# Scatter of the expert outputs issued behind the eight picks of a pass instead of directly behind the gather

## What is computed

```python
logits = xt @ w_router + b_router
top_v, top_i = lax.top_k(logits, 4); gates = softmax(top_v)
def expert_block(idx, gate, e):
    xb = xt[idx]                                   # gather of token rows
    g = min(xb @ w_gate[e] + b_gate[e], 7); u = clip(xb @ w_up[e] + b_up[e], -7, 7)
    y = (g * sigmoid(1.702 * g) * (u + 1)) @ w_down[e] + b_down[e]
    return y * gate
out = x + segment_sum(all blocks' y by token)      # scatter with addition
```

## Time and profile before

| | |
|---|---|
| time, median of 3 runs | 2278.34 us (2276.03 to 2282.03) |
| the profiled execution's own time | 2279.51 us |
| its span in the profile | 2277.8 us |
| PE busy | 96% of the span |
| DVE, ACT, POOL busy | 68%, 50%, 38% |
| from the gather of iteration 1 to the scatter behind the loop | 894.82 to 2212.10 us |

### The profile page before, as it was taken

One profiled execution on the slowest core, in us unless ns is written; L12 is line 12 of the kernel. 1 busy time (PEld: TensorE's weight loads), 2 busy tenths in 40 slices (PEclk: granted clock), 3 DMA queues, 4 the chain that ended last, 5 costly groups with the idle time before them and its releaser, 6 DMA issues.

```text
span 2277.8 us, 36180 instructions
## 1 busy us (share of the span) xinstructions
PE 2196.1 (96%) x11524; PEld 1552.7 (68%) x11525; DVE 1547.1 (68%) x1940; ACT 1128.4 (50%) x1130; POOL 857.1 (38%) x484
## 2 busy tenths in 40 slices
PE   8999999999999969999999999999999999999997
PEld 6874554787888747777666667666676766667775
DVE  5534443444344588888777878787788777788885
ACT  4432333423231145776555656565565565665664
POOL 1333120000000034656444555354555554455651
PEclk9999999999999979999999999999999999999999
DMA  6421111232333368999887888888898888798896
GB/s 233 90 76 46 46 37 29 75 101 84 100 113 130 131 261 276 362 337 333 299 285 271 295 304 305 291 310 302 303 333 294 295 299 302 269 303 319 323 336 193
DMA packets 206013, 517.82 MB, mean 227 GB/s; under 512 B 19168, under 2 KB 86624, under 8 KB 205952
## 3 DMA queue, kind: packets, MB, share of 16 engines
q1 hardware_dynamic: 190016, 470.97, 57.0%
q0 software_dynamic: 15936, 46.02, 9.4%
HBM read 480.68 MB, written 32.05 MB: 225 GB/s over the span
## 4 chain that ended last, share of the span: by engine, by line
PE 82%; DVE 7%; DMA 5%; issue 3%; ACT 2%; SPq 0%; POOL 0%; DVEq 0%; ACTq 0%; POOLq 0%
PE psum L1800 14%; PE psum L1802 12%; PE psum L1801 12%; PE psum L1623 7%; PE psum L1811 5%; DMA ring<-in_w_up 5%; PE psum L1645 4%; DVE w_lo L1336 4%; PE psum L1643 4%; PE psum L1644 4%; PE psum L1850 3%; PE psum L1567 2%; PE psum L1566 2%; PE psum L1568 2%; PE psum L1729 1%
## 5 line engine op out<-in xcount | busy, mean ns | idle before, releaser
L1336 DVE TENSOR_TENSOR w_lo<-ring,w_hi 128x2048 fp32r<-128x2048 f32 x384 | 874.8, 2301 | 110.1 <-ACT w_hi L882 98.9
L882 ACT ACTIVATE w_hi<-ring 128x2048 fp32r<-128x2048 f32 x384 | 728.5, 1920 | 370.9 <-DMA ring<-in_w_up 250.4
L646 POOL TENSOR_SCALAR pick<-iota_bf,slot_col 128x256 bf16<-128x256 bf16 x244 | 468.9, 1936 | 141.8 <-DVE slot_col L1349 141.8
L1800 PE MATMUL psum<-w_hi,xT_hi 128*128 128x512 f32 x1008 | 417.9, 415 | 29.7 <-DVE w_lo L1336 24.6
L1802 PE MATMUL psum<-w_hi,xT_lo 128*128 128x512 f32 x1008 | 401.7, 399 | 0.0
L1801 PE MATMUL psum<-w_lo,xT_hi 128*128 128x512 f32 x1008 | 401.4, 398 | 0.0
L1800 PEld LDWEIGHTS psum<-w_hi,xT_hi 128*128 128x128 f32 x1008 | 191.0, 189 | 142.4 <-issue 59.2
L652 POOL DMA_INDIRECT xg<-h_rows,idx_new x32 | 71.8, 2243 | 490.9 <-DVE idx_new L1330 473.3
L1800 PE MATMUL psum<-w_hi,aT_hi 128*128 128x512 f32 x528 | 221.3, 419 | 8.5 <-issue 4.5
L1802 PEld LDWEIGHTS psum<-w_hi,xT_lo 128*128 128x128 f32 x1008 | 191.6, 190 | 46.6
L1801 PEld LDWEIGHTS psum<-w_lo,xT_hi 128*128 128x128 f32 x1008 | 191.8, 190 | 39.8
(11 more groups left out here) (333 smaller groups left out, 3240.2 us busy)
## 6 DMA issues: line engine op xcount, KB each, us to landing
ring<-in_w_gate SPq DMA_DIRECT2D x256, 512.0 KB, 5.1
ring<-in_w_up SPq DMA_DIRECT2D x256, 512.0 KB, 6.4
ring<-in_w_down SPq DMA_DIRECT2D x256, 512.0 KB, 5.4
ring<-in_w_in SPq DMA_DIRECT2D x44, 512.0 KB, 5.1
ring<-in_x SPq DMA_DIRECT2D x16, 512.0 KB, 3.6
ring<-in_w_in SPq DMA_DIRECT2D x6, 1024.0 KB, 6.5
vb<-oT SPq DMA_DIRECT2D x16, 256.0 KB, 6.4
ring<-in_w_oc SPq DMA_DIRECT2D x16, 256.0 KB, 2.9
```

Source lines behind the costliest of these rows:

```text
L646: e.tensor_scalar(pick[:, t, :], iota_bf[:, :], slot_col[:, t, :], None, ALU.is_equal).then_inc(g_pick, 1)
L882: e.activation(w_hi[:, hs, :], ring[:, slot, :], ACT.Copy).then_inc(g_hi, 1)
L1336: e.tensor_tensor(w_lo[:, hs, :], ring[:, slot, :], w_hi[:, hs, :].bitcast(F32), ALU.subtract).then_inc(g_lo, 1)
L1800: e.matmul(dst, hi, w_up, start=start, stop=False)
```

## The change

POOL issues the scatter after the eight picks instead of between the gather and the picks. The wait for its landing and the raising of `g_free` follow directly. Two conditional blocks become one.

```diff
             with e.Fori(0, n_loop) as p:
                 gather(p + 2, False)
+                pick_tokens(p + 3)
                 with e.If(p > 0):
                     scatter(p)
-                pick_tokens(p + 3)
-                with e.If(p > 0):
                     scattered(p)
                 e.sem_inc(g_free, 1)
```

## The result

The changed kernel takes 2375.18 us (2372.24 to 2383.90, 4 runs) against 2278.99 us before: ratio 1.0425, 95% interval 1.0405 to 1.0445. It is 96 us slower. The prediction had the sign and the mechanism, but 17 us for the size, and a range that ended at 2321.

A forecast was written before the change was run, and what follows sets the result against it. PE was taken to bound the kernel, with 82% of the chain. Lateness of 19.7 us, less 7.0 for the removed collision, plus 4.3 for the clock, gave 17 us slower: 2295 us, range 2273 to 2321.

The forecast's parts named there:

- Where the loss would come from: At the pass end, DVE's `shift_rows` waits for `g_free` behind picks and scatter landing, delaying the next pass: 19.7 us.
- That the picks would not begin earlier: On POOL, picks still wait for `slot_col` and begin 14 to 15 us after the gather, so nothing is gained there.
- The hand-overs: Three steps, from picks to scatter and from landing over `g_free` to DVE, estimated at 0.9 us together.
- The landing of the pair: Both scatters issued and landed behind the picks in 8.4 us, taken from the scatter behind the loop; bounds 7.0 to 12.5.
- the subtraction of the prediction: POOL's idle time before each gather set against a 12.0 us chain; shortfalls, with the last pass, total 19.7 us.
- The room behind the picks: POOL's idle time before the next gather: 6.95 to 11.81 us in short passes, 12.79 or more in the others.
- the collision: Scatter packets delay weight loads in the first third of a pass; removing this was to give back 7.0 us.
- The clock: PE gaps at pass boundaries lower its granted clock; half of five shortfalls at 1.7 us each, 4.3 us.
- A longer chain: Rival: scatter issue or landing stretched behind the picks, 10.4 us for the pair; +47 us, 2325 us; chance 0.12.
- Faster: Rival: the pair lands within 5 us, nothing is late, PE's waits inside passes go; 2265 us; chance 0.14.
- just fits: Rival: the pair needs 7.0 us and hand-overs 0.6, lateness 9.0 against up to 12.5 gained; 2275 us; chance 0.18.
- The signs in the profile: Short passes become 42 to 43 us, long ones keep their length; PE's mid-pass waits shrink, ACT's `in_w_up` waits fall.

## Why the prediction was right in kind and wrong in size

- **Where the loss would come from.** Right: picks, issue, landing, `g_free`, `shift_rows`, and with it `row_numbers`, the gather and the first `w_lo`. The copy of the row numbers took that wait out and 86 of the 96 us with it.
- **That the picks would not begin earlier.** Right: 14.6 us after the gather.
- **The hand-overs, 0.9 us.** Too large. The scatter is issued 0.17 us behind the picks, and `shift_rows` starts within about 0.2 us of the landing.
- **The landing of the pair, 8.4 us. This step failed first.** In the pass shown it is 945.35 - 933.45 = 11.9 us up to the copy on DVE. I had taken the one scatter behind the loop for the nearest row, and set aside the landings of up to 9.7 us in the loop as being due to the gather ahead of them. With no gather ahead the median is 9.4 us, above that of before (7.7 us). So the queue behind the gather was not what made them long. The addition has about 2 us of it; what the rest is stays open. A fuller stream of loads is not shown: the DMA engines were as busy during the one scatter behind the loop, though they moved fewer bytes then (length, engines, PEclk, DMA share, GB/s; the kernel after, then before):

```profile
933.40:945.30 11.90, 4.84 (x36) 3.31 (x34) 1.12 (x2) 5.29 (x4) 3.21 (x2) 0.91 1.04 322
```

```profile
2212.10:2220.50 8.40, 8.40 (x37) 6.76 (x36) 8.05 (x6) 4.72 (x3) 3.53 (x2) 1.00 1.01 271
```

The need is then 0.2 + 11.9 + 2.7 = 14.8 us instead of 12.0. This pass is a fair sample: in the 13 late passes that a gather follows, it came 12.8 to 16.4 us behind the last pick, 14.8 on average. With that, the subtraction of the prediction over the idle times of before gives 51 us in 14 passes instead of 19.7 in eight.
- **The room behind the picks. The second step that failed.** I took it from the kernel before and made it smaller only where I credited a gain. But without the collision the short passes are shorter still, and most of them have longer picks: in the pass shown for the run without a scatter there are 6.88 us of room, where there were 13.71. Of the 107.2 us of waiting, this is the other half. In the 14 late passes the eight picks took 18.5 us on average, against 16.1 in the same passes of the kernel before: 33 us, which I had put at nothing. The relief (20.4 us by the run without a scatter, where I had counted 7.0 in the sum) could not show as time, because a pass in which the chain is the longest path can't use it; I count it as waiting on DVE. 51 + 33 + 20 = 104 us. The run without a scatter gives the same from the other side: its room falls short of 14.8 us in the same 14 passes, by 120 us together, and 2257.4 + 120 is 2377 us, where 2373.3 were measured.
- **The clock, 4.3 us.** Under-sized. PE's busy time in the loop grew by 12.7 us against before. The gaps at the boundaries were 5 to 11 us long, not 3 to 4. The granted clock was low for longer than the 3.4 us of the earlier trace rows: 0.66 as a mean over 15 us is about 10 us at the lower level. But more than half of that lay in the gap, where it costs nothing. The clock was low before PE began again at 949.50, and full by 954:

```profile
945.00:949.40 4.40, 0.00 (x0) 0.00 (x0) 3.76 (x14) 3.73 (x4) 1.37 (x1) 0.50 0.33 134
949.50:953.00 3.50, 3.50 (x8) 2.81 (x9) 3.15 (x2) 2.83 (x2) 3.19 (x2) 0.50 0.52 142
954.00:958.00 4.00, 4.00 (x19) 3.22 (x18) 3.69 (x3) 0.00 (x0) 0.00 (x0) 1.00 0.03 12
```

- **The rivals.** "A longer chain" was the case that came, with a price (2325 us) still too low, and already outside the stated range, which ended at 2321. It had assumed 10.4 us for the pair and unchanged picks. Of the two things that it named, the issue and the landing, only the landing was stretched: the issues took 2.18 and 1.87 us on average, against 2.54 and 1.84 in the loop before. "Faster" and "just fits" fell with the landing.
- **The signs in the profile.** The late passes became 45 to 50 us long, not 42 to 43; the other passes kept their length within 1.5 us, as forecast. The waits of PE of over 1.5 us inside a pass (four in the loop before) were gone. ACT's waits for `in_w_up` did not fall: in the loop they rose from 219 to 240 us. In pass 948.03 ACT waits 10.17 us for such a load, while the DMA engines are nearly idle from 954 to 958 us (0.03, above). I take it that these loads are issued late, because PE releases the slots late; this was not isolated.

In the ledger: 2277.8 us before, less 20.4 for the collision, plus 107.2 for DVE's waits, leaves 8.7 us to the 2373.3 us measured. Of these, 4.1 lie ahead of iteration 1, where neither kernel issues a scatter. By passes, the 88.5 us of the loop are 82 in the 14 late passes and 6.6 in passes directly behind a late one, at most 1.5 in each. The lower clock at their start is the likely cause of these 6.6; it was not isolated.

## What to carry to other kernels

Where an issue is moved, look for what its completion releases, and work out the chain up to the latest reader of that release, in the shortest pass and not in the mean one. Take the latency of a DMA from all its instances in the loop under load, not from the one instance behind it, and take the slack from a run in which the thing that you hope to remove is removed. If a late completion then holds several resources at once (here row numbers, output buffer and the issuing engine), free each of them by itself: a copy of 256 numbers, a wait moved behind the next gather, and the buffer's writer moved by two chunks turned a loss of 4% into a gain of 0.9%.

## What the runs showed of the hardware

- GpSimd's picks have no fixed length, and the trace shows what sets it. In the loop of the kernel after, 110 of the 232 picks start while DVE runs no `w_lo`, and 107 of these take 0.91 to 1.0 us. The other 122 start inside a `w_lo`; they take 2.48 to 4.82 us, and each ends at least 0.79 us behind that `w_lo`. The median is 2.50 us (before: 1.71), the mean 2.07 us (before: 1.92). The Trainium skill (SBUF — State Buffer, section "Who interferes with whom") says that a DVE instruction with two SBUF inputs contends with a GpSimd instruction that reads SBUF; `w_lo` and the pick are such a pair, and the trace agrees. One pick beside an instruction that reads PSUM, and the next pick, which begins 0.38 us into a `w_lo` that ends at 930.00:

```profile
926.59 1.21 DVE L1357 TENSOR_SCALAR ut<-psum 128x1024 f32<-128x1024 f32 x1
...
927.20 0.92 POOL L646 TENSOR_SCALAR pick<-iota_bf,slot_col 128x256 bf16<-128x256 bf16 x1
```

```profile
927.72 2.28 DVE L1335 TENSOR_TENSOR w_lo<-ring,w_hi 128x2048 fp32r<-128x2048 f32 x1
...
928.10 2.69 POOL L646 TENSOR_SCALAR pick<-iota_bf,slot_col 128x256 bf16<-128x256 bf16 x1
```

Even POOL's copy of 128 x 2 numbers took 0.18 us in one place and 1.83 us in another, where it began 0.5 us into a `w_lo` and ended with it. The first line is from POOL's timeline of the run with y_out later, the second from that of the run with the copy alone:

```profile
1020.78 0.18 POOL L660 COPY idx_out<-idx_cur 128x2 uint32<-128x2 uint32 x1 [4.92 <-ACT ys L930]
```

```profile
990.13 1.83 POOL L661 COPY idx_out<-idx_cur 128x2 uint32<-128x2 uint32 x1
```

- The addition in an indirect DMA took some 2 us of the 9.4 us from issue to landing of 128 rows of 1 KB, the second of a pair (7.5 us with plain writes).
- The issue of a scatter is held up in the same way. In the loop of the kernel after, 37 of the 58 issues start outside a `w_lo` and take 1.55 to 1.65 us, also beside `xT_lo`, which has one input in PSUM (933.45, above). The other 21 start inside one, end 1.43 to 1.51 us behind it, and take up to 3.71 us. In the kernel before, all 58 start inside a `w_lo` and take 2.54 and 1.84 us. So the 2.54 us of the earlier trace rows was not the price of the gather in front, and the pair's issues were not longer on average behind the picks. What grew was the time to the landing, which POOL's own busy time does not show. An issue that was held:

```profile
1265.68 2.29 DVE L1335 TENSOR_TENSOR w_lo<-ring,w_hi 128x2048 fp32r<-128x2048 f32 x1 [1.53 <-ACT w_hi L881]
1266.00 3.46 POOL L660 DMA_INDIRECT out_rows<-ys,idx_cur  x1 [0.17 <-issue]
```
